# The first block of Hyena's projection computed ahead of DeltaNet's scan, and the filter layers' small loads issued during it

## What is computed

```python
u_l = modulate(x, norm_g[i, 0], sh1, sc1) @ w_in[i]
ua_l, ub_l, uc_l, ud_l = jnp.split(u_l, splits, axis=-1)      # GLA, Hyena, Mamba, DeltaNet
...
def hyena_mixer(...):                                          # only the latent tokens are wanted
    uc = short_conv(u, conv_w, conv_b)                         # 3 taps, 768 channels
    v, x1, x2 = jnp.split(uc, [D_GROUP, 2 * D_GROUP], axis=-1)
    h = hyena_filters(l_, w1, b1, w2, b2, w3, b3, w4, freq)    # three small layers with sines, positions only
    z = x1 * long_conv(v, h[:, 0, 0], h[:, 0, 1], d[0])
    return x2 * long_conv(z, h[:, 1, 0], h[:, 1, 1], d[1])
```

## Time and profile before

| | |
|---|---|
| time, median of 3 runs | 1705.99 us (1704.48 to 1708.7) |
| profiled execution | 1710.0 us |
| its span, first to last instruction | 1708.1 us |
| mean granted TensorE clock | 0.941 |
| dn_s begins, hy_c begins | 595.96 us, 726.74 us |
| experts begin | about 1090 us |

### The profile page before, as it was taken

The page is one execution under the profiler, slowest core; times in us unless marked ns, Lnnn a source line. Parts: engine busy times, 40 slices in busy tenths (PEclk is TensorE's granted clock), DMA queues, the critical chain, the costliest instruction groups (busy, mean ns, idle before and its releaser), DMA issues. The chain is left out here.

```text
span 1708.1 us, 22349 instructions
## 1 busy us (share of the span) xinstructions
PE 1528.1 (89%) x8590; PEld 1238.7 (73%) x8590; DVE 1220.6 (71%) x1471; ACT 920.8 (54%) x1310; POOL 303.1 (18%) x371
## 2 busy tenths in 40 slices
PE   6899999988997789999999994399999999999991
PEld 3686788887776679877476783288888888888871
DVE  4873664296564667766799656788888888888873
ACT  5341354375547367643110563077777777777753
POOL 0300410070004786000000451001000110001001
PEclk9899999998998969999999996699999999999995
DMA  9571310032007733410411534299999999999957
GB/s 343 166 254 51 149 50 0 2 111 88 25 2 228 235 106 116 134 37 2 171 50 50 199 136 163 95 390 393 386 399 396 394 376 395 399 392 386 389 201 221
DMA packets 108141, 345.04 MB, mean 202 GB/s; under 512 B 36541, under 2 KB 46038, under 8 KB 83459
## 3 DMA queue, kind: packets, MB, share of 16 engines
q1 hardware_dynamic: 98622, 320.34, 49.6%
q0 software_dynamic: 5328, 18.88, 4.6%
q10 hardware_dynamic: 4085, 4.40, 1.0%
HBM read 301.01 MB, written 37.32 MB: 198 GB/s over the span
## 5 line engine op out<-in xcount | busy, mean ns | idle before, releaser
L3773 DVE TENSOR_TENSOR w_lo<-w_raw,w_hi 128x2048 fp32r<-128x2048 f32 x192 | 438.3, 2292 | 64.4 <-ACT w_hi L3715 64.3
L3715 ACT ACTIVATE w_hi<-w_raw 128x2048 fp32r<-128x2048 f32 x192 | 368.0, 1917 | 146.9 <-PE ps L3660 133.5
L3658 PE MATMUL ps<-w_hi,xsT_hi 128*128 128x512 f32 x512 | 202.6, 396 | 0.2 <-DVE xsT_lo L3778 0.2
L3660 PE MATMUL ps<-w_hi,xsT_lo 128*128 128x512 f32 x512 | 200.2, 391 | 0.0
L3659 PE MATMUL ps<-w_lo,xsT_hi 128*128 128x512 f32 x512 | 200.0, 391 | 0.0
L3626 POOL DMA_INDIRECT moe_sum<-y,idx_col x15 | 30.6, 2043 | 460.9 <-ACT y L3735 460.9
L3658 PEld LDWEIGHTS ps<-w_hi,xsT_hi 128*128 128x128 f32 x512 | 96.5, 188 | 20.0 <-DVE xsT_lo L3778 0.9
L3660 PEld LDWEIGHTS ps<-w_hi,xsT_lo 128*128 128x128 f32 x512 | 96.3, 188 | 20.2
L3659 PEld LDWEIGHTS ps<-w_lo,xsT_hi 128*128 128x128 f32 x512 | 96.5, 188 | 19.3
L3658 PE MATMUL ps<-w_hi,hiddenT_hi 128*128 128x512 f32 x256 | 99.8, 390 | 0.6 <-DVE hiddenT_lo L3790 0.6
L3659 PE MATMUL ps<-w_lo,hiddenT_hi 128*128 128x512 f32 x256 | 99.7, 390 | 0.0
(11 more groups left out here) (622 smaller groups left out, 3632.6 us busy)
## 6 DMA issues: line engine op xcount, KB each, us to landing
w_raw<-in_moe_w_gate SPq DMA_DIRECT2D x64, 1024.0 KB, 6.8
w_raw<-in_moe_w_up SPq DMA_DIRECT2D x64, 1024.0 KB, 8.4
w_raw<-in_moe_w_down SPq DMA_DIRECT2D x64, 1024.0 KB, 8.6
w_mod_row<-in_w_mod SPq DMA_DIRECT2D x32, 512.0 KB, 4.9
w_mod<-in_w_mod SPq DMA_DIRECT2D x8, 1024.0 KB, 17.6
dn_ma<-dn_ma SPq DMA_DIRECT2D x16, 512.0 KB, 4.6
dn_mT<-dn_ma SPq DMA_DIRECT2D x20, 256.0 KB, 4.0
x_tile<-in_x SPq DMA_DIRECT2D x8, 512.0 KB, 15.8
```

Source lines behind the costliest of these rows:

```text
L3658: nc.tensor.matmul(out, h[:, kk, :], wh[w][:, c:c + 512], start=kk == 0, stop=False)
L3660: last = nc.tensor.matmul(out, l[:, kk, :], wh[w][:, c:c + 512], start=False, stop=kk == KD - 1)
L3715: nc.scalar.activation(wh[q % RING][:, :], S.raw[q % RAW][:, :], ACT.Copy).then_inc(s.hi, 1)
L3773: nc.vector.tensor_tensor(wl[q % RING][:, :], S.raw[q % RAW][:, :], wh[q % RING][:, :].bitcast(F32), ALU.subtract).then_inc(s.lo, 1)
```

## The change

Block 0 of Hyena's projection is computed in dn_a, behind TensorE's last unit:

- ScalarE's queue loads the block's weights (512 KB) after the last gate copy; ScalarE rounds them, VectorE subtracts for the low part before it takes over the substitution;
- TensorE: 32 products with the high weights, of which those for classes 1 and 4 come last and wait for `moved`; then 16 with the low weights; then `keep_busy` with 12 products in place of 24, in bank 0;
- ScalarE copies the two banks (128 x 1024) to `hy_first_line`, ahead of its wait for the inverse and its load of blocks.

In hy_c, `start` is 1: weights are split by quarters for block 1; block 0 has two small products instead of its 48 and is "evacuated" from `hy_first_line`; banks alternate the other way (`bank`); `ahead` is 2, so the norm's transposes come after block 1; the filter's first product comes after block 1's first chunk. The 21 small loads of the filter layers are issued by SyncE in the scan, in step 6, ahead of that step's attention load. The filter's single tap goes to banks 2 and 3.

```diff
@@ project_conv @@
+    start = 0 if first is None else 1
+        def bank(i, c):
+            return 3 * ((i + start) % 2) + c
...
-        ahead = 2 if part and lat[0] and lat[1] else 1
+        ahead = 2 if first is not None or part and lat[0] and lat[1] else 1
...
             for i, b in enumerate(blocks):
+                if i < start:
+                    for c in mine[i]:
+                        nc.tensor.matmul(S.ps[:, 7, 0:256], S.t("ident"), S.tab[:, 0:256], start=True, stop=True
+                                         ).then_inc(s.prod, 1)
+                    continue
...
                     last.then_inc(s.prod, 1)
+                    if i == start == 1 and c == mine[i][0]:
+                        side.pe(s, pe, 0)
...
-                if weights and i + 1 < NB:
+                if weights and start < i + 1 < NB:
...
-                    src = S.ps[:, 3 * (i % 2) + c, 0:n]
+                    src = S.ps[:, bank(i, c), 0:n] if i >= start else first[:, t0 - CTX:t0 - CTX + n]
@@ deltanet, dn_a, TensorE @@
             pe.wait_ge(s.kbc_a, N - HEAD)
-            keep_busy(nc, S, 6, 24)
+            pe.wait_ge(s.og_out, LT - OG_AHEAD)
+            pe.wait_ge(s.hy_hi, 1)
...
+            for c in range(2):
+                for k in (0, 2, 3, 5, 6, 7, 1, 4):
+                    if k == 1:
+                        pe.wait_ge(s.moved, 32)
+                    nc.tensor.matmul(pair(c), hw_high[:, k, :], high(k, c), start=(k == 0), stop=False)
+                    nc.tensor.matmul(pair(c), hw_high[:, k, :], low(k, c), start=False, stop=False)
+            pe.wait_ge(s.hy_lo, 1)
+            for c in range(2):
+                for k in range(KD):
+                    last = nc.tensor.matmul(pair(c), hw_low[:, k, :], high(k, c), start=False, stop=(k == KD - 1))
+            last.then_inc(s.hy_prod, 1)
+            pe.wait_ge(s.mt, N - 1)
+            keep_busy(nc, S, 0, 12)
@@ dn_a, ScalarE @@
+                        if g == LT - 1:
+                            nc.scalar.dma_start(hw[:, :, :], A["w_in"][0, :, HY0:HY0 + P].rearrange("(p k) n -> p k n", p=P)
+                                                ).then_inc(s.hy_in, 16)
...
+            act.wait_ge(s.hy_in, 16)
+            nc.scalar.activation(hw_high[:, :, :], hw[:, :, :], ACT.Copy).then_inc(s.hy_hi, 1)
+            act.wait_ge(s.hy_prod, 1)
+            act.wait_ge(ma_st[(N - 1) % DN_RING], stored((N - 1) % DN_RING, N))
+            nc.scalar.activation(S.hy_first[:, :], S.ps[:, 6:8, :].rearrange("p a b -> p (a b)"), ACT.Copy).then_inc(s.hy_out, 1)
             act.wait_ge(s.zeroed, 1)
             act.wait_ge(s.d_st, 16)
             load_blocks(nc.scalar, 0, 1)
@@ dn_a, VectorE @@
+            dve.wait_ge(s.hy_hi, 1)
+            nc.vector.tensor_tensor(hw_low[:, :, :], hw[:, :, :], hw_high[:, :, :].bitcast(F32), ALU.subtract).then_inc(s.hy_lo, 1)
             dve.wait_ge(s.sub, 1)
             substitute(nc.vector, Chain(dve, s.chain), bd, HANDED).then_inc(s.sub, 1)
@@ dn_s, SyncE @@
                 load_mt(sp, st)
+                if st == 6:
+                    S.filter.load_small(sp)
                 if st - 1 >= 4:
                     sp.wait_ge(s.av, 2 * (st - 1) - 2 - NX)
```

More of the change, by code:

```diff
@@ L593, in split_high @@
         def split_high(act, i):
-            for j in QUARTERS if i == 0 else (None,):
-                if i == 0:
+            for j in QUARTERS if i == start else (None,):
+                if i == start:
                     act.wait_ge(weights[j], 16)
@@ L708, in _ @@
             if weights:
-                split_high(act, 0)
+                split_high(act, start)
             if part:
@@ L790, in _ @@
             if weights:
-                split_low(dve, 0, range(3))
-                norm.dve(s, dve, ch, lambda: split_low(dve, 0, range(3, 4)))
+                split_low(dve, start, range(3))
+                norm.dve(s, dve, ch, lambda: split_low(dve, start, range(3, 4)))
             elif part and lat[0]:
@@ L1881, in deltanet @@
     plan = Plan(nc, mark)
-    with Stage(nc, "dn_a", "r_in*5 e0 e kb kb_v kbt kbc kbc_a em em_v kk qk mt at og og_out zeroed cleared taken sub d_st moved chain pchain") as s:
+    with Stage(nc, "dn_a", "r_in*5 e0 e kb kb_v kbt kbc kbc_a em em_v kk qk mt at og og_out zeroed cleared taken sub d_st moved chain pchain "
+                            "hy_in hy_hi hy_lo hy_prod hy_out") as s:
         R = [plan.take(f"dn_rel{i}", [P, HEADS, P]) for i in range(5)]
@@ L2740, in pe @@
         if i == 0:
[L2741 removed]
+            pe.wait_ge(self.small, 21 * 16)
         else:
@@ L2813, in hyena @@
                            by_class=True))
-    side = FilterLayers(nc, A, Plan(nc, S.norm_end))
+    side = S.filter
     side.ps = S.ps
@@ L2821, in hyena @@
     line, conv = project_conv(nc, S, A, "hy_c", blocks, Plan(nc, SBUF_END - 384 - CONV_BYTES), norm, side, ctx=False,
-                              weights=S.hy_w, later=True)
+                              weights=S.hy_w, later=True, first=S.hy_first)
     assert side.end <= SBUF_END - 384 - CONV_BYTES
@@ L3198, in _ @@
             result(1)
-    SPENT.extend([fwd_in, win_in, y_back, w_out_in] + S.hy_w)
+    SPENT.extend([fwd_in, win_in, y_back, w_out_in, S.filter.small] + S.hy_w)
 HALF_AT = 32
```

52 lines of the change are left out of this document (32 added, 20 removed).

## The result

The changed kernel takes **1717.62 us** (median, 1714.8 to 1721.84) against 1705.99 before: ratio **1.0061**, 95% interval 1.004 to 1.0081. By the ratio it is slower by 10.4 us (the medians differ by 11.6); the forecast was 1709.0, its range 1700 to 1716. The profiled execution has a span of 1715.8 us (before 1708.1), at a mean clock of 0.938.

What follows compares the result with a forecast made beforehand. It found TensorE busy 89% of the span, with GpSimd's chain ending dn_a and VectorE's chain limiting hy_c's gain. Terms 4.7 - 1 + 1.5 - 2.2 = +3.0 us gave 1713.0, or 1709.0 on the median's footing; range 1700 to 1716.

Steps and rivals of the forecast that it cites:

- The small loads in SyncE's queue: Scan: 21 loads in step 6 make step 7's dn_mT 0.9 us late; +1.5 us, bounds 0 and +3.5.
- rival B: Scan, step 7's dn_mT: SyncE's queue holds the scan, costing 5 to 6 us, total 1713; chance 0.25.
- the clock behind a wait in dn_a and in hy_c: TensorE at half clock after waiting: up to 1.7 us more in dn_a's tail, +1.0 in hy_c.
- The tail of dn_a: End of dn_a: products waiting for moved copies, then fillers, make TensorE end the stage instead of GpSimd; +4.7 us.
- the bound of 5.5: End of dn_a: the tail's cost in all if the clock stays at half for 3.3 us after the wait.
- The scan behind a busy TensorE: Scan's start: TensorE busy right before it may keep the clock up; taken as -1 us, bounds nothing and 7.6.
- Rival C: Scan's start: full clock holds into 602 to 618, 6 us come back, total 1704; chance 0.18.
- hy_c: Hyena's projection without block 0: -3.2 us for block 2's earlier start, +1.0 for low clock; together -2.2 us.
- block 2 26.5 us behind the start: hy_c: block 2 starts earlier, 24.5 to 28 us behind the stage's start, before 29.7.
- a gap of TensorE of 6 to 7 us: hy_c: TensorE waits before block 0's transposes, released by ScalarE; 6 to 7 us.
- Rival D: hy_c gives all 11.0 us less 1 us of fillers, tail and scan cancel: 1696; chance 0.10.
- The parts at nothing: dn_a: weights' load, ScalarE's rounding and VectorE's 1.22 us subtraction lie under a 4.9 us cover; cost nothing.

Runs made afterwards that it cites:

- e2_fill_step6: Changed kernel plus 5 filling products in step 6 of the scan, ahead of the wait for step 7's dn_mT: 1717.2 us, ratio 1.0068.
- e1: Changed kernel with the 21 small loads spread over seven steps of the scan, three a step: 1713.75 us, ratio 1.0041.
- e9: Changed kernel with the small loads back at the start of hy_c, so only the block moved: 1716.03 us, ratio 1.0061.
- e12: As e9, with two quarters of Hyena's weights loaded behind step 8's dn_diag and dn_mT: 1712.86 us, ratio 1.0043.
- e3: Kernel before with only the small loads moved, all into step 6 of the scan: 1717.87 us, ratio 1.0064.
- e10: Kernel before with only the small loads moved, spread over seven steps of the scan: 1704.13 us, ratio 0.9996.
- e13: Kernel before with two quarters of Hyena's weights loaded behind step 8's blocks, nothing else: 1702.65 us, ratio 0.9982.
- e5: As e1, with dn_a's 36 products that need no moved copy first and 6 filling products for 12: 1705.77 us, ratio 0.9989.
- e8: Changed kernel with loads spread, dn_a's tail reordered, weight quarters last in step 8 and hy_c in the new order: 1698.78 us, ratio 0.9951.
- e11: As e8, with the small loads back at the start of hy_c: 1706.21 us, ratio 0.999.
- e6_hyc_order: As e4, with hy_c reordered: norm's transposes earlier, norm's copies and block 0's finish before the sine, VectorE's split before the convolution: 1701.49 us, ratio 0.9963.
- e4: As e1, with the 12 filling products at the end of dn_a taken out: 1707.45 us, ratio 1.0002.

## Why the prediction was wrong, point by point

**The small loads in SyncE's queue: the failed step.** The mechanism and its place were right, but the term for SyncE's queue was 1.5 where 8.9 was measured, and rival B's 5.5 was short too. Two things were mis-sized. One is the lateness: dn_mT left 82.14 us behind the scan's start in place of 81.14 (21 loads took 13.9 us and not 13.2, the two loads behind them 2.1 and not 1.9), it landed 4.7 us after and not 4.0, and TensorE waited 2.65 us and not 0.9. The other is the price of a wait: I let a microsecond of wait cost a microsecond. The prediction did count the clock behind a wait in dn_a and in hy_c, at 1.7 and 1.0, but not here, where it costs most: 4.9 us by e2_fill_step6. In the scan the clock took 14 us to come back. The Trainium skill (TensorE: Matmul & The Clock Gate, HAM oscillation — how this bites in real kernels) describes this, a wait for a transfer after which TensorE is throttled again; the trace agrees, with 1.00 before the wait and 0.50 behind it.

**The tail of dn_a: right in kind, somewhat small.** Forecast +4.7, the profile has +4.0. The agreement is partly luck: 0.9 of the forecast stood for a clock that falls behind the wait of 3.3 us, and in this execution it did not fall. In e2_fill_step6, behind a wait as long (3.33 us), it was at 0.50. The windows behind the two waits (after, then e2_fill_step6):

```profile
583.20:591.60 8.40, 8.40 (x36) 6.84 (x37) 6.60 (x22) 0.00 (x0) 0.96 (x2) 1.00 0.43 166
583.70:588.00 4.30, 4.30 (x10) 3.43 (x11) 3.85 (x14) 0.00 (x0) 0.00 (x0) 0.50 0.77 299
```

Over five profiles with this tail (after, e1, e2, e9, e12) dn_a is 87.3 to 91.7, mean 89.5; over four without the block (before, e3, e10, e13) it is 81.5 to 85.4, mean 83.4. So the term is nearer +6. The end of dn_a follows two things: the landing of the moved copies, 72.6 to 75.3 us behind the stage's start, and the clock behind the wait. From that landing to the fillers TensorE needs 8.4 us in after, near the 8.2 forecast at full clock, and 11.0 in e2_fill_step6, where the clock costs more than the 1.7 that I gave it at most. In all eight profiles TensorE goes on 6.2 to 6.3 us behind the copies' issue, so what varies is when SyncE issues them. I had dated the landing from one execution, near the early end (72.7), and the bound of 5.5 was too low. In the reordered tail (e5, e8, e11) the mean is 84.1.

**The scan behind a busy TensorE: right in direction, and smaller.** Forecast -1. Measured: the 1st `z` 10.81 us behind the start (before 11.27), so -0.5; the 4th at 51.48 (before 51.63), so -0.2 is left. The clock was 0.50 from 6 us on, as before:

```profile
603.00:619.00 16.00, 15.20 (x134) 13.33 (x136) 7.54 (x18) 8.88 (x31) 14.20 (x24) 0.50 0.24 53
```

Rival C needed 1.00 there. Later profiles have the fast start, without the block too (e10_small_spread), so the fast start doesn't need the block; and in e9_block_only step 8 took its gain back.

**hy_c: right.** Forecast -2.2, measured -2.1; block 2 26.5 us behind the start, measured 26.3; a gap of TensorE of 6 to 7 us, measured 5.0, released by ScalarE's norm copies. Rival D, that the block simply comes off, falls with that gap, but e6_hyc_order shows that 9.0 of its 10 us in hy_c were to be had in another order.

**The parts at nothing.** Right: the load, ScalarE's rounding and VectorE's subtraction (1.58 us and not 1.22) lay under waits.

**What the sum could not hold.** The halves don't add. By the ratios they cost 10.9 us (e3) and 10.4 (e9) alone, and 10.4 together. A scan that has already been held up for step 7 comes late enough to step 8 that it doesn't wait there, and small loads issued in the scan take away the wait of 6.45 us in hy_c. In the trace the scan's term makes up the gap between forecast and measurement. Taking that loss away alone (e1_spread) showed only 3.9 us of it in the timed runs. The wait of step 8 and a longer tail of dn_a could hold the rest in those executions; that is argued and not shown.

## What to carry to other kernels

Before work is put into a queue that feeds a loop, reckon for each load of the loop how late it may be, and price a late load by the clock as well as the wait: in the scan of this kernel, waits of 1 to 3.3 us went with 7.2 to 9.5 us lost over two steps (after, e3, e4, e6, e9). Moving work off a stage pays once the stage's other chains are put in order for it; look for what stands behind a wait and would be ready (here the norm's copies behind the sine, and products that need no moved data behind those that do). Test the halves of a change alone and together, since one may be the condition of the other.

## What the runs showed of the hardware

- **The clock came back at different speed.** In the scan of after, behind 2.65 us of wait, TensorE was busy 2.00 of 2 us and stayed at 0.50 from about 684 to 697.5; in hy_c, behind 4.95 us of wait, it was back at 1.00 after 4.3 us of work (761.54 to 765.85). The Trainium skill (TensorE: Matmul & The Clock Gate, Part 1) says that activity releases the throttle; both rows agree that the clock comes back under work, one of them after 14 us only.
- **The length of the wait did not decide whether the clock fell.** It fell behind 0.97 us in e9_block_only and 3.33 us in e2_fill_step6's dn_a. It stayed at 1.00 behind 3.38 us in after's dn_a, and behind 0.76 us that followed filling products in e2_fill_step6's scan. The scan's first three steps, equal in code, took 35.0 us at a mean clock of 0.89 (e9_block_only) and 40.4 at 0.69 (before).
- A small load cost SyncE's queue 0.66 us (13.9 for 21), single ones up to 1.37 us. The Trainium skill (DMA: Bandwidth & Descriptors, Rules for kernel authors) has it that small transfers pay mostly overhead; here that overhead was the queue's time.
